# RWKV recurrence of a ten-stage fp32 trunk: a pair's scores and masks one turn earlier, third and second buffers in the weight slots, modulation rows moved to later stages

## What is computed

```python
mod = silu(c) @ ada_w[i] + ada_b[i]                       # six rows of 1024 for each layer i
sh1, sc1, g1, sh2, sc2, g2 = split(mod, 6)
h = rms(x) * (1 + sc1) + sh1
y = rwkv7_mix(h, ...)                                     # 16 heads of 64, see below
x = x + g1 * y
h = rms(x) * (1 + sc2) + sh2
x = x + g2 * swiglu(h, ffn_w_gu, ffn_w_down)

def rwkv7_step(state, (r, w, k, v, a, b)):                # 64x64 state of each head, 512 steps
    sa = state @ a
    state = state * w + outer(sa, b) + outer(v, k)
    y = state @ r
```

## Time and profile before

| what | us |
|---|---|
| median of 3 runs (2794.64 to 2798.92) | 2795.52 |
| the profiled execution | 2793.61 |
| its span, first to last instruction | 2791.7 |
| TensorE matmul busy | 2578.8 (92%) |
| VectorE busy | 1194.2 (43%) |
| ScalarE busy | 981.7 (35%) |
| GpSimd busy | 955.0 (34%) |

### The profile page before, as it was taken

How to read it: one execution, slowest core, us unless ns; L and a number is a source line. 1 busy time by engine, 2 the same in 40 slices (tenths; PEclk the granted TensorE clock), 3 DMA queues, 4 the chain that set the end, 5 groups by cost and what they waited for, 6 DMA issues and landing times.

```text
span 2791.7 us, 33786 instructions
## 1 busy us (share of the span) xinstructions
PE 2578.8 (92%) x14024; PEld 2007.7 (72%) x14024; DVE 1194.2 (43%) x1794; ACT 981.7 (35%) x1446; POOL 955.0 (34%) x334
## 2 busy tenths in 40 slices
PE   7996676779999988998999999989899999999999
PEld 5755665368887867876887878868687777777686
DVE  5465875854343353344111343434306424343604
ACT  4652443323322233443332333222324334433523
POOL 2312121433444433443444433413433333222232
PEclk8997988889999999999999999999999999999999
DMA  6113443024555421112222332202122222111121
GB/s 259 65 71 104 129 110 86 31 76 158 194 189 194 152 91 69 53 66 80 96 90 104 136 126 94 102 31 91 39 105 77 94 79 103 61 46 54 45 92 61
DMA packets 93396, 272.10 MB, mean 97 GB/s; under 512 B 54864, under 2 KB 54992, under 8 KB 65488
## 3 DMA queue, kind: packets, MB, share of 16 engines
q1 hardware_dynamic: 91248, 265.52, 27.1%
q10 hardware_dynamic: 2016, 4.72, 0.5%
HBM read 264.44 MB, written 5.78 MB: 97 GB/s over the span
## 4 chain that ended last, share of the span: by engine, by line
PE 77%; DVE 11%; ACT 4%; DMA 3%; issue 3%; POOL 2%; SPq 1%; ACTq 0%; DVEq 0%; POOLq 0%
PE bank L342 20%; PE bank L344 19%; PE bank L343 19%; PE bank L278 2%; PE bank L276 2%; PE bank L277 2%; PE bank L2614 1%; PE bank L3139 1%; DMA inverse<-scratch_inverse 1%; POOL ring_low L373 1%; ACT w_high L363 1%; DVE conv_out L2340 1%; PE bank L2860 1%; PE bank L3127 1%; DVE probs L3336 1%
## 5 line engine op out<-in xcount | busy, mean ns | idle before, releaser
L373 POOL TENSOR_TENSOR ring_low<-ring,w_high 128x2048 fp32r<-128x2048 f32 (+2 forms) x184 | 800.8, 4354 | 1348.4 <-ACT w_high L363 1348.4
L342 PE MATMUL bank<-h_high,w_high 128*128 128x512 f32 (+1 forms) x1304 | 523.3, 401 | 28.3 <-DVE h_low L453 20.0
L344 PE MATMUL bank<-h_high,ring_low 128*128 128x512 f32 (+1 forms) x1304 | 520.2, 399 | 0.0
L343 PE MATMUL bank<-h_low,w_high 128*128 128x512 f32 (+1 forms) x1304 | 517.5, 397 | 0.0
L363 ACT ACTIVATE w_high<-ring 128x2048 fp32r<-128x2048 f32 (+2 forms) x184 | 330.9, 1801 | 389.2 <-PE bank L344 373.1
L342 PEld LDWEIGHTS bank<-h_high,w_high 128*128 128x128 f32 (+1 forms) x1304 | 247.1, 189 | 94.5 <-issue 27.4
L343 PEld LDWEIGHTS bank<-h_low,w_high 128*128 128x128 f32 (+1 forms) x1304 | 246.9, 189 | 60.6 <-issue 0.7
L344 PEld LDWEIGHTS bank<-h_high,ring_low 128*128 128x128 f32 (+1 forms) x1304 | 246.6, 189 | 60.3
L342 PE MATMUL bank<-z_high,w_high 128*128 128x512 f32 x384 | 154.3, 402 | 12.5 <-DVEq L1859 6.4
L344 PE MATMUL bank<-z_high,ring_low 128*128 128x512 f32 x384 | 153.8, 400 | 0.0
L343 PE MATMUL bank<-z_low,w_high 128*128 128x512 f32 x384 | 152.8, 398 | 0.0
(11 more groups left out here) (440 smaller groups left out, 4479.6 us busy)
## 6 DMA issues: line engine op xcount, KB each, us to landing
ring<-in_stream SPq DMA_DIRECT2D x210, 1024.0 KB, 4.8
ada_slot<-in_ada_next SPq DMA_DIRECT2D x48, 512.0 KB, 3.2
scale_weights<-in_first SPq DMA_DIRECT2D x4, 1024.0 KB, 19.1
inverse<-scratch_inverse SPq DMA_DIRECT2D x16, 256.0 KB, 4.4
w_first<-in_first SPq DMA_DIRECT2D x2, 1024.0 KB, 7.6
x_res<-in_x SPq DMA_DIRECT2D x2, 1024.0 KB, 12.0
scratch_rows<-scores SPq DMA_DIRECT2D x16, 128.0 KB, 2.6
x_res<-in_x ACTq DMA_DIRECT2D x1, 2048.0 KB, 8.3
```

The costliest lines, as they stand in the source:

```text
L342: pe.matmul(out, w_high[:, k, cols], x_high, start=start, stop=False)
L343: pe.matmul(out, w_high[:, k, cols], x_low, start=False, stop=False)
L344: return pe.matmul(out, w_low[:, k, cols], x_high, start=False, stop=stop)
L373: pool.tensor_tensor(self.c.ring_low[:, b % SLOTS, 0:cols], self.c.ring[:, b % SLOTS, 0:cols], self.high_buf[:, b % 2, 0:cols].bitcast(F32 ...
```

## The change

Three things are changed; nothing of the arithmetic is.

1. In the recurrence each pair is spread over three parts of the loop in place of two. Turns run from -1 to 9; turn p makes keys, scores and masks of pair n = p + 1, solves the blocks of pair p, does the levels of pair q = p - 1, and the results of pair o = p - 2. The scores `SC` and values `UV` get a third buffer and the inverses `XY` a second; they lie in weight slots 1 to 3, which the recurrence no longer uses for weights. SyncE issues the next pair's score transfers after the reads of the current inverse.
2. Slot 0 is the recurrence's only modulation slot: 8 loads of two tiles, one in each turn, 16 tiles (sh2, sc2) in place of 32.
3. The 8 tiles of g1 move to the output stage: two loads of 2 MB are issued by ScalarE at its start, and VectorE sums them between the last gate and the first residual. The 8 tiles of g2 move to the feed-forward, whose 56 tiles now all lie in the 22 steps: three in each of the first 12, two in each of the other 10.

The diff, cut to its core:

```diff
+    ada_slot = chip.over("ada_slot", [P, SLOT], F32, chip.ring_offset)
+    spare = chip.ring_offset + 4 * SLOT
+    SC.append(chip.over("scores_2", [P, 2, NC_, 3 * CHUNK], F32, spare))
+    UV.append(chip.over("u_v_2", [P, NC_, 2, CHUNK], F32, spare + 24 * NC_ * CHUNK))
-    XY = chip.keep("inverse_16", [P, 2, NS, CHUNK])
+    XY = [chip.keep("inverse_16", [P, 2, NS, CHUNK]),
+          chip.over("inverse_16", [P, 2, NS, CHUNK], F32, spare + 32 * NC_ * CHUNK)]
...
     def tensor(pe):
+        def first_product(q):
+            X = XY[q % 2]
+            inv_in.wait(pe, q)
+            level.wait(pe, q, 1)
+            if q + 1 < KD:
+                a_out.wait(pe, q + 1)
+                v_out.wait(pe, q + 1)
+            both(4, 5, lambda k, par, h, c: pe.matmul(
+                to(k, par, h, c), Lm[rows(par), system(h, c), :], X[rows(par), 0, system(h, c), :],
+                start=True, stop=True), t1_mm)
+
+        def results(q):
+            y2_out.wait(pe, q)
+            t1_out.wait(pe, min(q + 1, KD - 1))
+            r_out.wait(pe, min(q + 2, KD - 1))
+            t2_out.wait(pe, q)
+            outer(q, 0)
+            outer(q, 1)
...
+        for p in range(-1, KD + 2):
+            n, q, o = p + 1, p - 1, p - 2
+            A, B, C = n < KD, 0 <= q < KD, 0 <= o
+            if B:
+                first_product(q)
+            if C:
+                results(o)
             if A:
+                keyed.wait(pe, n)
+                if C:
+                    n_out.wait(pe, o)
+                    o_out.wait(pe, o)
...
+                scores(n, 0)
+                if C:
+                    g_out.wait(pe, o)
+                    r_add.wait(pe, o)
+                scores(n, 1)
...
+                keys(n)
             if B:
+                X = XY[q % 2]
                 t1_out.wait(pe, q)
                 if A:
+                    masked.wait(pe, n)
...
     def vector(dve):
+        for p in range(-1, KD + 2):
+            n, q, o = p + 1, p - 1, p - 2
+            A, B, C = n < KD, 0 <= q < KD, 0 <= o
+            solves = 0 <= p < KD
+            if solves:
+                solve_blocks(p)
+            if C:
+                y1_out.wait(dve, o)
+                merge(o, y2_mm, y2_out, Y1, Y1, 2)
+            if solves:
+                solve_corner(p)
+            if A:
+                key(n)
+            if C:
+                for par in range(2):
+                    g_out.wait(dve, o, par)
+                    r = systems(f.r, o)[:, par:NC_:2, :]
+                    dve.tensor_tensor(r, bank(2 + par, P)[:, :, CHUNK:P], r, ALU.add).then_inc(r_add.sem, 1)
+            if A:
+                mask(n)
+            if solves:
+                next_ada(p)
             if B:
+                X = XY[q % 2]
                 if q:
                     t2_mm.wait(dve, q - 1)
+                merge(q, x1_mm, x1_out, X1, X[:, 0, :, :], 0)
                 if q:
                     wu_mm.wait(dve, q - 1)
+                merge(q, y1_mm, y1_out, Y1, X[:, 1, :, :], 2)
...
     def sync(sp, phase):
...
+        def turn(p):
             masked.wait(sp, p)
...
+            if p:
+                ada_sum.wait(sp, p - 1)
+            sp.dma_start(ada_slot[:, :], chip.io["first"][6 + p]).then_inc(ada_in.sem, 16)
+
+        turn(0)
+        for p in range(KD):
             solved.wait(sp, p)
...
+            if p + 1 < KD:
+                turn(p + 1)
+        ada_sum.wait(sp, KD - 1)
+        gr_mm.wait(sp, KD - 3)
+        no_mm.wait(sp, KD - 3)
+        y1_out.wait(sp, KD - 1)
```

ScalarE's order in a turn becomes: evict the first product of q, evict the results of o, `grow(n + 1)`, evict keys, rows and values of n, t2 of q, r of n. GpSimd's program is unchanged. The output stage and the feed-forward:

```diff
 def rwkv_output(chip):
     def scalar(act):
         act.dma_start(chip.x[:, :, :], chip.io["x"].rearrange("(k p) t -> p k t", p=P)).then_inc(x_back.sem, 16)
+        for n in range(2):
+            act.dma_start(g1[n][:, :, :], chip.io["g1"][n]).then_inc(g1_in[n].sem, 16)
...
         dve.sem_inc(chip.gemm_done, 2)
+        for n in range(KD):
+            dve.wait_ge(g1_in[n // 4].sem, g1_in[n // 4].landed)
+            ada_tile(chip, dve, g1[n // 4][:, n % 4, :], 2 * KD + n).then_inc(g1_sum.sem, 1)
+        dve.wait_ge(g1_sum.sem, g1_sum.of(KD - 1))
+        ada_finish(chip, dve, 2 * KD, 3 * KD, ada_biased, ada_one_plus)
...
 def ffn(chip, layer):
+    def ada_here_of(n):
+        return range(3 * n, 3 * n + 3) if n < 12 else range(2 * n + 12, 2 * n + 14)
...
             for n in range(KF):
                 up(n // 4, n % 4)
-                next_ada(2 * n)
-                next_ada(2 * n + 1)
+                for t in ada_here_of(n):
+                    next_ada(t)
...
-            if ada_next and n < 48 - 2 * KF:
-                next_ada(2 * KF + n)
...
     def sync(sp, phase):
...
-            for t in here:
+            for t in ada_here_of(n - 3) if 3 <= n < KF + 3 else ():
                 if t:
                     sp.wait_ge(ada_sum.sem, ada_sum.of(t - 1))
                 sp.dma_start(ada_slot[:, :], chip.io["ada_next"][t]).then_inc(ada_here, 16)
```

More of the change, by code:

```diff
@@ L104, in __init__ @@
         ring_offset = self.top
+        self.ring_offset = ring_offset
         self.ring = self.keep("ring", [P, SLOTS, SLOT])
@@ L1287, in outer @@
                         mm.then_inc(wu_mm.sem, 1)
-        for p in range(KD + 1):
-            q = p - 1
-            A, B = p < KD, p >= 1
-            if A:
[L1293 to L1304, removed]
-            if B:
[L1306 to L1317, removed]
-                if p >= 2:
-                    u_out.wait(pe, p - 2)
-                    w_out.wait(pe, p - 2)
-                elif p:
-                    bk_out.wait(pe, 0)
-                keys(p)
-            if B:
@@ new lines, in first_product @@
+        def first_product(q):
[15 more added lines that the diff above has]
+            outer(q, 1)
+            u_out.wait(pe, q)
+            bk_out.wait(pe, q)
+            for n in range(2):
+                for c in range(NC_):
+                    for h in range(2):
+                        keys_t, uv = SC[q % 3][:, h, c, 0:CHUNK], UV[q % 3][:, c, h, :]
+                        reads = SC[q % 3][:, h, c, CHUNK:2 * CHUNK]
+                        mm = pe.matmul(bank(n, CHUNK)[rows(h), c, :], keys_t if n == 0 else uv,
+                                       uv if n == 0 else reads, start=True, stop=True)
+                mm.then_inc(no_mm.sem, 1)
+            w_out.wait(pe, q)
+            for n in range(4):
+                for h in range(2):
+                    for par in range(2):
+                        c = 2 * n + par
+                        mm = pe.matmul(chip.bank[2 + par][rows(h), n * P:(n + 1) * P],
+                                       W[rows(par), system(h, c), :], SC[q % 3][rows(par), h, c, 0:P],
+                                       start=True, stop=True)
+                        if n == 3 and h == 1:
+                            mm.then_inc(gr_mm.sem, 1)
@@ L1341, in tensor @@
+                if B:
+                    t1_out.wait(pe, q)
+                rows_and_values(n)
             if B:
@@ L1605, in vector @@
-            if A:
-                solve_corner(p)
-            if p + 1 < KD:
-                key(p + 1)
-            if A:
-                next_ada(2 * p + 1)
-            if B:
-                for par in range(2):
-                    g_out.wait(dve, q, par)
-                    r = systems(f.r, q)[:, par:NC_:2, :]
-                    dve.tensor_tensor(r, bank(2 + par, P)[:, :, CHUNK:P], r, ALU.add).then_inc(r_add.sem, 1)
+                merge(q, y1_mm, y1_out, Y1, X[:, 1, :, :], 2)
         def decay_of(g, c):
```

244 lines of the change are left out of this document (107 added, 137 removed).

## The result

The changed kernel took 2893.78 us (median of 4 runs, 2892.0 to 2895.94) against 2795.65 us for the kernel before beside it (2794.64 to 2798.92): a ratio of 1.0349, 95% interval 1.0331 to 1.0367, slower by 98 us. The profiled execution took 2893.07. The forecast was 2860 in a range of 2820 to 2894: right in sign and range, but 0.2 us from the range's far end and 34 us too low. One execution in the experiments, of the run with the merge first, took 11270 us and is left out of that run's ratio.

A forecast was written before the change was run, and what follows sets the result against it. The prediction saw a closed loop across engines bounding the recurrence and TensorE pacing the feed-forward beside a single tile slot. Recurrence -7.8, output stage +0.9 and feed-forward +72 made +65: 2858.7, with 1.9 added 2860 us; range 2820 to 2894.

The forecast's parts named there:

- What bounds the feed-forward: Feed-forward: three tiles through one slot take 13.8 us, over TensorE's step of 11.17; the stage was forecast at +72 us.
- Steps and their two lengths: Feed-forward, three-tile steps: 14.95 us if the tile's sum starts before GpSimd's rounding, 18.3 if the rounding starts first.
- The odds of the race: Feed-forward: tile against GpSimd's rounding for first start; tile loses half to two thirds, +72 us, ends 25 and 103.
- rival 1: Feed-forward: GpSimd's rounding always starts before the tile's sum; +103 us, 2892 us in all; chance 0.2.
- rival 3: Feed-forward: the third tile hides, needing a wait under 2.5 us; only -6.9 is left, 2789 us; chance 0.08.
- The output stage: Output stage: two more DMA issues on ScalarE cost +0.9 us; VectorE's eight tiles delay the first residual 1.4, costing 0.
- The recurrence: Recurrence: the new order gives turns of 23.7 us and a gain of 7.8 us, ends 17 and 0.
- The rows: Recurrence: rows of scores go out and back, so the block solve starts 6.1 us after the masks' end.
- The level products: Recurrence: GpSimd's two products per pair, 2.61 us each, lie beside corner and key and alternate with VectorE's two-SBUF-input products.
- small solve steps: Recurrence: VectorE's short steps of the block solve, before the merge of the inverse's second half; taken as 3.3 us.
- the results take 10.1 us: Recurrence: TensorE's products for a pair's results, taken as 7.46 us, ending 18.8 us after the masks' end.
- rival 4: Recurrence: it gives nothing or 17 us, moving any other case 8 up or 9 down; no chance of its own given.

## Why the prediction was right, and where it was short

The mechanism that made the loss, one slot in the feed-forward, was the predicted one. That the time lies inside the range is luck: all the larger errors below go the same way, the median is 0.2 us inside, and two of the four executions lie outside.

- **What bounds the feed-forward.** Right: one slot, and TensorE made to wait through GpSimd's rounding. Two slots took the loss away whole.
- **Steps and their two lengths.** Right: 17.8 to 18.4 us measured for a step with three tiles against 18.3 worked out, 13.3 to 13.9 against 13.7 for two, and the first step 13.74 against 13.66. The two that the tile won took 14.47 (14.95 worked out) and 9.83 (10.35).
- **The odds of the race. This is the mis-sized term.** The prediction let the tile lose "half to two thirds of the races" and took 72. It lost 19 of 21: the twelve steps cost 76 us and all of it 95. Its rival 1 (always lost, +103, 2892) came nearest, and had a chance of 0.2. GpSimd starts 3.23 to 3.34 us behind the product, nearly always 3.33; the tile's sum starts 3.20 to 4.46 behind it, and one race was lost by 0.01 us. The prediction had the numbers for this, and set the wrong two against each other. It held the waits of the earlier trace rows against 3.35, and 9 of the 21 waits before are indeed below that. But a wait is counted from the end of the sum's tiny second instruction, 0.08 us behind the start of the product (the two rows at 655.15 above). So the waits have to be under about 3.26, and of the 21 only three are (3.17, 3.24 and 3.25). The side of a race on which most of the waits stand is the side to price it at.
- **The third tile does not hide** (rival 3). Right: no tile landed within 2.5 us of its issue; the quickest took 3.07.
- **The output stage.** +0.9 forecast, +0.6 measured; the eight tiles there cost nothing, though the first residual came 4.4 us later behind the last add and not 1.4.
- **The recurrence.** Wrong in sign: -7.8 forecast, +3.0 measured. Three terms of the turn failed together, seen in the turn shown above. The rows take 7.2 us, not 6.1. The level products were placed beside corner and key, since TensorE's first product was to end 10.1 us behind the masks; it ends 8.2 behind, and they lie beside the small solve steps, which take 5.7 us, not 3.3 (the run with a second level buffer shows that this counts: -10 us). And the results take 10.1 us, not 7.46, because TensorE idles 6.16 us before them and then runs at its lower level (in the run with added products, with that time filled, the first 32 take 1.96 us again). The prediction took durations from turns in which these three were undisturbed. Its own rival 4 had the recurrence giving 0 at worst. It also counts eight tiles fewer in the recurrence; the change takes out sixteen.
- **The order.** The prediction took the merge behind the solve and the keys behind the corner as given, and counted on results and keys running side by side. No dependence asks for either. With both moved the turn falls from 25.9 to 24.1 us with one level buffer, and from 23.9 to 21.6 with two. The merge moved alone, with one buffer, made it longer.

## What to carry to other kernels

Before more loads go through a single buffer, compare (round trip + use) x loads with the time of the step that hides them; over it (13.8 us against 11.17 here) the loads are on the path, and here a second buffer took away 97 us, all but 1 of the loss. In a loop spread over engines, ask of each instruction on the fullest in-order queue whether it needs what stands ahead of it: here four key products and two merges, moved ahead of a solve that they did not need, took off 23 us with the port cleared. And move one of them alone only with the ring worked out: the merge by itself cost 6, because it has to wait for TensorE and what stands behind it then waits too.

## What the runs showed of the hardware

- A VectorE product that meets a GpSimd instruction waits for its end: products of 0.24 to 0.32 us took 1.0 to 1.1 beside GpSimd instructions of 1.3 us. So a row of short instructions can lose something at each instruction of GpSimd. GpSimd loses too: its pair of level products took 4.33 us in place of 2.6 where they met the 1.2-us modulation sums (row below, run with the keys first).
```profile
372.49 4.33 POOL L1665 TENSOR_TENSOR level<-scores,const 64x512 f32<-64x512 f32 x2 [14.66 <-DVE scores L1595]
...
373.42 2.28 DVE L653 SCALAR_TENSOR_TENSOR ada_slot<-ada_slot,c_row 128x1024 f32<-128x1024 f32 x1
```
- In the changed kernel TensorE idled 2.2 to 8.0 us ahead of the results of six pairs, and the 32 products behind that took 3.4 to 3.7 us. With 1.8 us of idle time or less they took 1.96, the upper level (2.4 GHz), in most turns, but not for the last pair (3.59 us behind 1.56 of idle time). In the run with a second level buffer 2.5 us of idle time came once before 1.96 us and once before 3.42. So the length of the idle stretch alone does not say which level follows. The granted clock over three of the turns was 0.81 to 0.93; in the run with added products it was 1.00.
- Landing of a 512 KB tile hardly moved with two under way: the median is 3.3 us with one slot and 3.4 to 3.5 in the run with two. It is the time from issue to landing that the single slot paid for, once for each tile.
